# A two-layer decoder step: extra expert rows turned one chunk ahead, and the last layer's expert rows summed in PSUM

## The reference

```
x = x + y                                        # mixer
h = rms_norm(x, g_ffn)
gp = softmax(h @ w_rg + b_rg); g_val, g_idx = top_k(gp, 1)        # 1 of 4 groups
e_val, e_idx = top_k(softmax(logits of that group), 2)            # 2 of its 8 experts
act = silu(h @ w_gate[e]) * (h @ w_up[e]) * weight[e]             # D_EXPERT = 256
x = x + act @ w_down[e], summed over the two experts
...
y = x * rsqrt(mean(x * x) + 1e-6) * g_final      # after layer 1
```

## Time and profile before

| | us |
|---|---|
| median of three runs | 1174.64 (1173.73 to 1178.26) |
| the profiled execution's own time | 1172.26 |
| its span (first to last instruction) | 1170.5 |
| TensorE busy | 1029.1 (88%) |
| VectorE busy | 427.6 (37%) |
| granted TensorE clock, mean | 0.949 |

### The profile page before, as it was taken

The page is one execution under the profiler, slowest core; times in us unless marked ns, Lnnn a source line. Parts: engine busy times, 40 slices in busy tenths (PEclk is TensorE's granted clock), DMA queues, the critical chain, the costliest instruction groups (busy, mean ns, idle before and its releaser), DMA issues.

```text
span 1170.5 us, 19147 instructions
## 1 busy us (share of the span) xinstructions
PE 1029.1 (88%) x7027; PEld 653.9 (56%) x7028; DVE 427.6 (37%) x904; ACT 209.6 (18%) x425; POOL 183.3 (16%) x282
## 2 busy tenths in 40 slices
PE   5999998879899978788399999988999998899980
PEld 4888786545555544444177767644565554555540
DVE  2542002454721111111349899454462111112116
ACT  4000112232201110011230101163120111111112
POOL 1000010000043222121112120110013222222120
PEclk9999999989999998899799999999979999999995
DMA  9424032345489999999642200264068999999915
GB/s 358 203 102 158 1 125 74 135 189 209 156 295 409 408 409 409 409 409 414 280 182 73 72 1 1 62 257 162 18 256 289 406 407 403 390 402 408 382 70 230
DMA packets 73776, 281.61 MB, mean 241 GB/s; under 512 B 12830, under 2 KB 13406, under 8 KB 70304
## 3 DMA queue, kind: packets, MB, share of 16 engines
q1 hardware_dynamic: 56992, 251.53, 54.8%
q0 software_dynamic: 10960, 17.89, 4.4%
q10 hardware_dynamic: 5744, 11.10, 2.8%
HBM read 270.23 MB, written 29.65 MB: 256 GB/s over the span
## 4 chain that ended last, share of the span: by engine, by line
PE 62%; DMA 20%; DVE 12%; ACT 3%; issue 2%; ACTq 0%; POOLq 0%; SPq 0%; POOL 0%; DVEq 0%
DMA ring<-w_moe 12%; PE psum L2137 11%; PE psum L2041 7%; DMA ar<-w_moe 6%; PE psum L2198 6%; PE psum L1812 5%; PE psum L1768 5%; PE psum L2234 5%; DVE ar L1671 5%; PE psum L2259 3%; PE psum L1881 2%; DVE X L1395 2%; PE psum L2120 2%; PE psum L2167 2%; PE psum L1879 1%
## 5 line engine op out<-in xcount | busy, mean ns | idle before, releaser
L2137 PE MATMUL psum<-ring,ar 128*64 128x256 f32 x1408 | 176.9, 396 | 18.2 <-DMA ring<-w_moe 16.3
L2137 PEld LDWEIGHTS psum<-ring,ar 128*64 128x64 f32 x1408 | 101.7, 142 | 89.9 <-issue 26.3
L2234 PE MATMUL psum<-ar,ring 128*128 128x272 f32 x512 | 121.3, 398 | 5.3 <-DVE ar L1657 2.9
L2234 PEld LDWEIGHTS psum<-ar,ring 128*128 128x128 f32 x512 | 97.6, 192 | 30.2 <-issue 4.2
L1671 DVE SCALAR_TENSOR_TENSOR ar<-ar,sv 128x512 f32<-128x512 f32 x120 | 107.0, 893 | 5.8 <-ACT ar L1025 1.9
L1601 DVE COPY ar<-psum 128x128 f32<-128x128 f32 x64 | 18.7, 292 | 245.0 <-PE psum L2188 245.0
L2041 PE MATMUL psum<-ring,ar 128*128 128x512 f32 x192 | 90.6, 622 | 4.7 <-DVE ar L1385 4.7
L2137 PE MATMUL psum<-ar 128*64 128x256 f32 x640 | 81.5, 399 | 8.1 <-DMA ar<-w_moe 8.1
L2198 PE MATMUL psum<-ring,ar 128*64 128x512 f32 x352 | 84.1, 598 | 0.8 <-DVE ar L1601 0.4
L742 POOL DMA_INDIRECT expert_outputs<-ar,ixy x64 | 63.9, 998 | 55.4 <-POOL ixy L739 55.4
L2137 PEld LDWEIGHTS psum<-ar 128*64 128x64 f32 x640 | 45.9, 143 | 42.4 <-issue 12.1
(11 more groups left out here) (262 smaller groups left out, 1188.2 us busy)
## 6 DMA issues: line engine op xcount, KB each, us to landing
ring<-w_moe SPq DMA_DIRECT2D x44, 2048.0 KB, 16.6
ring<-w_moe SPq DMA_DIRECT2D x44, 1024.0 KB, 18.1
ar<-w_moe SPq DMA_DIRECT2D x20, 2048.0 KB, 16.5
ar<-w_moe SPq DMA_DIRECT2D x20, 1024.0 KB, 17.1
ring<-w_pw SPq DMA_DIRECT2D x6, 2048.0 KB, 10.6
ring<-w_mix SPq DMA_DIRECT2D x3, 3072.0 KB, 23.9
ring<-expert_outputs SPq DMA_DIRECT2D x8, 1024.0 KB, 7.8
ring<-kv_in SPq DMA_DIRECT2D x2, 2880.0 KB, 11.3
```

The costliest lines, as they stand in the source:

```text
L2137: t = mm(psum[64 * f:64 * f + 64, u % 2, 0:2 * P], xt[:, k, 64 * (u % 2):64 * (u % 2) + 64], w[:, k, f, :], start=k == 0, stop=k == KD - 1)
L2234: t = mm(psum[:, glu_bank(m) + h, 0:HALF], w[:, k, o:o + P], hT2[:, k, HALF * h:HALF * h + HALF], start=k == 0, stop=k == KD - 1)
```

## The change

Five edits are made together; the letters are those of the prediction, where D stands for two of them.

A. The loads of the start all go out on SP's queue, in the order in which they are used: tile 0, the identity, tile 1, the gains, tile 2, the first weights, tiles 3 and 4, further weights, and then the rest of constants and small vectors, which have semaphores of their own.

B and C. The rows of an extra chunk are turned one chunk ahead. The first chunk's are turned before job 1's products in each layer (`turn_more_rows(0)`), whether there is a chunk or not, and chunk c + 1's in the middle of chunk c. `keep_more_rows` is VectorE's part. Pool gathers one chunk further ahead and moves the clearing and the gather of the third pair of jobs behind the first chunk's. The chunk's intermediate tiles move to the router weights' place, its transposed product to another bank.

D. Before layer ends: Pool no longer copies an index where it is known when the program is built (the last eight jobs), ScalarE reads its counts ahead of the waits, and the fetch of tile 0 is split in two, with a semaphore for each half.

E. After layer 1, TensorE sums residual and expert rows in PSUM: identity times `X`, plus two diagonal matrices of the weights (made by VectorE) times the expert rows. ScalarE and VectorE read the sum there for the norm. Eighteen fill products stand ahead of the wait for `all_out`.

```
-            sp.dma_start(cst[:, :], consts).then_inc(consts_in, 16)
-            sp.dma_start(sv[:, :], smalls).then_inc(smalls_in, 16)
+            tokens_in(0)
+            sp.dma_start(cst[:, 0:C_SM], consts[:, 0:C_SM]).then_inc(ident_in, 16)
+            tokens_in(1)
+            sp.dma_start(sv[:, 0:V_GPK], smalls[:, 0:V_GPK]).then_inc(gains_in, 16)
+            tokens_in(2)
             sp.dma_start(ring[:, 0, 0:2 * D], w_mix0[0, :, 0:2 * D]).then_inc(later_w[0], 16)
+            tokens_in(3)
+            tokens_in(4)
...
@@ Pool, experts(n)
                 first_rows(1)
-                nc.gpsimd.memset(xg[2], 0.0).then_inc(moe.rows_clear, 1)
-                first_rows(2)
                 nc.gpsimd.memset(xe, 0.0).then_inc(pool_link, 1)
...
                 pool.indirect_dma_start(xe, None, xn_dram, ...).then_inc(ex[n].rows, 16)
+                nc.gpsimd.memset(xg[2], 0.0).then_inc(moe.rows_clear, 1)
+                first_rows(2)
                 rows_of(3, 6)
+                pool.wait_ge(ex[n].turned, 2)
+                nc.gpsimd.tensor_copy(ixe[0:JOB, 0:1], tg[0:JOB, MORE + 1:MORE + 2]).then_inc(ex[n].index, 1)
+                pool.wait_ge(ex[n].index, 2)
+                pool.indirect_dma_start(xe, None, xn_dram, ...).then_inc(ex[n].rows, 16)
...
-                            chunk_rows(before + c + 1)
+                            chunk_rows(before + c + 2)
                             chunk_out(before + c)
...
@@ Pool, outputs(it, u, known)
+                    if known:
+                        index = tb[:, MSLOTS * it + u:MSLOTS * it + u + 1]
+                        pool.wait_ge(moe.y_kept, MSLOTS * it + (EXPERTS * n + u + 1))
...
@@ SP, fetch(n)
+                    if i == 0:
+                        sp.dma_start(yg[0][:, 0:D], src[:, 0:D]).then_inc(first_rows_in, 16)
+                        sp.dma_start(yg[0][:, D:], src[:, D:]).then_inc(tile_in[0], 16)
...
@@ ScalarE, experts(n)
+                further_chunks, before_last = (act.value_load(...) for o in (EXPERTS - 1, 2 * EXPERTS - 1))
                 for b in range(3):
                     act.wait_ge(moe.y_out[b], 16 * (n + 1) * len(range(b, EXPERTS, 3)))
-                further_chunks, before_last = (act.value_load(...) for o in (EXPERTS - 1, 2 * EXPERTS - 1))
                 act.wait_ge(ex[n].out, 16 * (before_last + further_chunks) + 16)
                 act.sem_inc(moe.all_out, 1)
@@ VectorE
+                def keep_more_rows(chunk):
+                    dve.wait_ge(ex[n].turned, chunk + 2)
+                    nc.vector.tensor_tensor(xeT, psum[:, 7, :] ..., gains, ALU.mult).then_inc(ex[n].turns_kept, 1)
...
+                            if first and u == 1:
+                                keep_more_rows(0)
                             further(it, u - 1)
@@ TensorE, experts(n)
+                def turn_more_rows(chunk):
+                    pe.wait_ge(ex[n].rows, 16 * chunk + 16)
+                    pe.sem_inc(moe.seen, 1)
+                    rows_ = xe.rearrange("t (d k) -> t k d", k=KD)
+                    for k in range(KD):
+                        t = tr(psum[:, 7, JOB * k:JOB * k + JOB], rows_[:, k, :], ident[0:JOB, 0:JOB])
+                    t.then_inc(ex[n].turned, 1)
...
                             t.then_inc(ex[n].gu, 1)
+                            pe.wait_ge(moe.rows_kept, ...)
+                            turn_more_rows(before + c + 1)
                             pe.wait_ge(ex[n].act, before + c + 1)
...
                             t.then_inc(ex[n].down, 1)
+                            pe.wait_ge(ex[n].turns_kept, before + c + 2)
...
                             down_weights(it, u - 1)
+                            if first and u == 1:
+                                turn_more_rows(0)
+                                pe.wait_ge(ex[n].turns_kept, 1)
                             further(it, u - 1, 4 if jobs == MSLOTS else 1)
@@ TensorE, the end
+            def residual(i):
+                r = ROWS[i]
+                for h in range(2):
+                    mm(psum[0:r, 2 * (i % 4) + h, :], ident[0:r, 0:r], X[0:r, i, 512 * h:512 * h + 512],
+                       start=True, stop=False)
+            def expert_rows(i):
+                r = ROWS[i]
+                for k in range(2):
+                    if i == 0 and k == 0:
+                        pe.wait_ge(first_rows_in, 32)
+                    else:
+                        pe.wait_ge(tile_in[i], 48)
+                    pe.wait_ge(moe.combined, TILES + 2 * i + k + 1)
+                    for h in range(2):
+                        o = D * k + 512 * h
+                        t = mm(psum[0:r, 2 * (i % 4) + h, :], weight_diag(i, k), yg[i][0:r, o:o + 512],
+                               start=False, stop=k == 1)
+                t.then_inc(moe.last_sums, 1)
+            residual(0)
+            residual(1)
+            pe.wait_ge(moe.y_kept, 2 * EXPERTS)
+            residual(2)
+            stay_warm(18, 7)
+            pe.wait_ge(moe.all_out, 2)
+            residual(3)
+            for i in range(TILES - 1):
+                expert_rows(i)
+            pe.wait_ge(y_ready, 1)
+            residual(4)
+            expert_rows(4)
@@ VectorE, the end
-            update = combine(1)
-            update(0)
...
+                for k in range(2):
+                    nc.vector.tensor_scalar(weight_diag(i, k), ident[0:r, 0:r],
+                                            cw[0:r, ODD_ORDER.index(i), k:k + 1], None, ALU.mult
+                                            ).then_inc(moe.combined, 1)
...
-                nc.vector.scalar_tensor_tensor(out=view(D * i, D, parts=r), in0=X[0:r, i, :],
+                nc.vector.scalar_tensor_tensor(out=view(D * i, D, parts=r), in0=last_sum(i),
```

More of the change, by code:

```diff
@@ L702, in chunk_rows @@
                     pool.wait_ge(ex[n].turned, chunk + 1)
-                    o = nc.s_assert_within(chunk + MORE, MORE, 2 * MORE,
-                                           skip_runtime_bounds_check_because="at most MORE chunks and one empty")
-                    nc.gpsimd.tensor_copy(ixe[0:JOB, 0:1], tg[0:JOB, bass.ds(o, 1)]).then_inc(ex[n].ix, 1)
-                    pool.wait_ge(ex[n].ix, chunk + 1)
+                    o = nc.s_assert_within(chunk + MORE, MORE, 2 * MORE + 1,
+                                           skip_runtime_bounds_check_because="at most MORE chunks and two empty")
+                    nc.gpsimd.tensor_copy(ixe[0:JOB, 0:1], tg[0:JOB, bass.ds(o, 1)]).then_inc(ex[n].index, 1)
+                    pool.wait_ge(ex[n].index, 2 * chunk - 1)
                     pool.sem_inc(moe.seen, 1)
@@ L749, in body @@
                             rows_of(3 * it + (u // 2 + 4), u + 8)
-                        outputs(it, u)
+                        outputs(it, u, not gathers)
                 first_rows(0)
@@ L806, in _ @@
         def _(act):
-            for i in range(TILES):
-                act.dma_start(X[0:ROWS[i], i, :], x_in[P * i:P * i + ROWS[i], :]).then_inc(tile_in[i], 16)
             links = [0]
@@ L1390, in update @@
                     r = ROWS[i]
[L1391 removed]
+                    if i == 0:
+                        dve.wait_ge(first_rows_in, 16 * (n + 1))
+                    else:
+                        dve.wait_ge(tile_in[i], 16 * (n + 2))
                     for k in range(2):
+                        if i == 0 and k:
+                            dve.wait_ge(tile_in[0], 16 * (n + 2))
                         if k:
```

140 lines of the change are left out of this document (78 added, 62 removed).

## The result

The changed kernel takes 1183.2 us in the median (22 runs) against 1175.9 for the kernel before beside it (22 runs): a ratio of 1.0064, 95% interval 1.0047 to 1.0081, so 7.5 us (5.5 to 9.5) slower. Forecast was 1175.5 us, 0.9 us above the kernel before, with a range up to 1183.0. The time missed the range by 0.2 us. One of the 22 runs took 1812.6 us at a granted clock of 0.55; the ratio leaves it out, and without it the median is 1183.0, the very end of the range. The difference is clearer: the interval lies wholly above 1, and 0.64% is more than the 0.5% that the prediction took as the least that can be told from no change. "Same" had been its likeliest outcome.

The account below looks back on a forecast made before the run. The chain of waits was taken to run through TensorE nearly everywhere, with exceptions at the start, layer 0's expert weights and after each layer's experts. Terms -2.4 + 4.4 - 11.1 - 1.3 + 11.3 = +0.9 us gave 1175.5, range 1168.5 to 1183.0.

Parts of the forecast that it names:

- A: Start of the kernel: loads reordered on one queue bring the first projection sooner, -2.4 us (-4.5 to -0.5).
- B: Job 1 of both layers: turning the first extra rows there costs +2.4 and +2.0, together +4.4 us (+4 to +8).
- C: Layer 1's extra chunks: rows turned one chunk ahead make chunks shorter, -11.1 us (-13 to -9).
- D: End of layer 0: earlier register loads gain 1.06 us, the dropped index copy 0.25, the split fetch nothing; -1.3 us.
- E: End of layer 1: sums and fill on TensorE take 41.2 us after the last down products, +11.3 us (+10 to +12.5).
- Same: Outcome that the whole kernel's time cannot be told from no change, within about 0.5% (5.9 us); chance 0.72.
- rival 3: End of layer 1: the fill is hidden under the fetch, expert rows start 11.8 us earlier, 1163.7 us; chance 0.05.
- rival 2: Layer 1's chunks: their gain is lost to weights whose stream ends 9.6 us later than forecast, 1186.6 us; chance 0.05.
- ScalarE, not the DMA, sets the pace: Start, after tile 0's square: about 2.9 and 2.76 us to the third square, at 9.9 instead of 13.06 us.
- The price is what the same pair costs inside a chunk: 1.97 us: First turn before job 1, both layers: from first transpose to next product it takes 1.97 us, as in a chunk.
- Rival 1: Job 1 of both layers: TensorE waits on Pool's late gather, 6.5 us more than forecast, 1182.0 us; chance 0.10.
- Nothing gained, up to 0.4 lost: End of layer 0, split fetch: VectorE begins 1.2 us earlier, but its second tile comes no sooner, at about 578.6 us.

Follow-up runs that it names:

- e1: Changed kernel without its 18 fill products at the end of layer 1: 1174.2 us, ratio 0.9983 to the kernel before.
- e2: Changed kernel with the last layer's sums back on VectorE, the rest of the change kept: 1168.8 us, ratio 0.9945 to the kernel before.
- e6: Kernel before with the changed start alone, and tile 3 of X loaded ahead of the first weights: 1176.8 us (one run, beside 1178.2).
- e3: Changed kernel with TensorE's wait for the first extra rows' copy moved behind job 1's gate products: 1178.0 us, ratio 1.0022 to the kernel before.
- e4: Changed kernel with the first extra rows turned behind job 1's gate products: 1178.1 us, ratio 1.0034 to the kernel before.
- e5: Kernel of e2 with the first tile's rows fetched in one piece again, both layers: 1174.1 us, ratio 0.9970 to the kernel before.
- the three combined kernels: c1, c2 and c3: 1164.7, 1165.5 and 1160.0 us.
- e7: Changed kernel with fill products around the first turn of extra rows, two ahead and five behind: 1187.1 us, ratio 1.0114 to the kernel before.
- e8: The changed kernel measured again, unaltered, beside e7: 1180.4 us, ratio 1.0050 to the kernel before.
- c1: Changed kernel with last sums on VectorE, one-piece fetch, TensorE's copy wait behind job 1's gate products, tile 3 first: 1164.7 us, ratio 0.9900.
- c2: As c1, with Pool clearing the extra rows' buffer before it waits for the job table: 1165.5 us, ratio 0.9905 to the kernel before.
- c3: As c1, but with e4's order of the first turn in place of e3's: 1160.0 us, ratio 0.9886 to the kernel before.

## Why the prediction was wrong, point by point

- **E, the end of layer 1 (+11.3 forecast): right.** +11.2 and +10.7 in two profiles, 36 rows of fill, nothing idle on TensorE, first sum 22.1 us after the end of the last down products, where 22.7 was forecast; the last instruction ends 41.2 us after it, as forecast. e1 and e2 show the cause from both sides, and rival 3, a hidden fill, falls with them.
- **C, the chunks (-11.1): right.** Single chunks 7.06 us where 7.24 was forecast. The whole stretch from job 1's down products of layer 1 to the last is 11.9 and 10.2 us shorter. TensorE waits for no weights from 950 us on, so rival 2 falls.
- **A, the start (-2.4): mis-sized.** -1.15 and -1.47. The step that failed is "ScalarE, not the DMA, sets the pace". It was followed to tile 2 only, and there it held but for 0.8 us (10.70 us where 9.9 was forecast). Tile 3 behind 1 MB of weights was left out, and VectorE runs in order: a late reciprocal for tile 3 holds back tile 2's multiply. e6 moves that one load and gets -2.63. The term as a whole, -1.2 and -1.5, still lies in its own range (-4.5 to -0.5).
- On the Trainium skill's "Issuing engines are not separate DMA queues" (DMA: Bandwidth & Descriptors), weighed in the prediction as a possible result of nothing: e6's -2.63 us speaks against it as a rule about A. The order of the loads is what changed, and it was worth 2.3 to 2.8 us right (four profiles), 1.1 to 1.6 with one load too late (eight). That the queue they are issued from has a share in it is not excluded: no run changes it alone.
- **B, the first turn (+4.4): too small, the largest miss.** Layer 0 +3.7 and +3.5 (forecast 2.4), layer 1 +6.4 and +3.9 (forecast 2.0). The step that failed is "The price is what the same pair costs inside a chunk: 1.97 us". From the first transpose to the next product it was 3.25 us in layer 0 (330.47 to 333.72) and 3.02 in layer 1. In a chunk the next product follows the copy at once. Ahead of job 1 stand the register load of the chunk count and the branch, in TensorE's queue behind the wait, and with them it is 1.2 to 1.4 us from the copy's end to the product (e3). To it comes a gather a little late in layer 1 (0.6 us of waiting, where none was forecast; in layer 0 none, where 0.4 was), and in some executions the half clock behind the gap, 1.4 to 2.6 us. The part of B on which I was right is that layer 0's shift goes to the layer's end in full: +3.4 us at job 0's down products, +3.7 at the last (in e3 and e4, what was taken off there came back in part on the way). Rival 1 named the right place and the wrong wait: it is the copy and what is queued behind it, more than the gather.
- **D, the end of layer 0 (-1.3): did not arrive.** +0.1 and 0.0. The fetch was issued 0.85 us sooner after the last down products than before; it would have been 1.4, but the last output's DMA took 3.71 us instead of 3.15. Then the split, costed at "Nothing gained, up to 0.4 lost", made tile 1 late by as much: it landed 8.2 us after the first issue, where the prediction has 7.2 (571.38 to 578.6). Without the split, e5 and the three combined kernels are at -0.3 to -0.6 us, so the split is not all. In e3, e4 and e7 the split is kept and the last output's DMA takes 2.4 us; TensorE's first transposes come 1.3 to 1.4 us sooner than before, yet the first product only 0.4 to 0.6. What TensorE gained at its first transposes went in the fill behind them, as told under e5. The prediction had no such term: whatever came sooner for VectorE had still to pass through TensorE's queue.

Sum of the terms as measured in the quieter profile (e8): A -1.5, B +3.5 and +3.9, C -10.2, D 0, E +10.7, together +6.3 us, against medians of +7.5 and +5.9. The forecast of +0.9 had C and E right and lost 1 us on A, 3 on B and 1.3 on D. The range's upper end lay 8.4 us above the 1174.6 that it was made against. The measured difference, 7.5 us, is inside that, and the median of 1183.2 outside by 0.2, which is chance; but the likeliest value was wrong by 6.6 us, and "same" was wrong with it. The misses on A, B and D are of one kind: something queued in order behind what moved.

## What to carry over

A wait that is put ahead of a register load and a branch costs these too: price it from the wait's end to the next real instruction, not from the same pair elsewhere. When a load is moved in a queue, follow the chain past the first consumer, to the instruction that stands next in order on each engine. And fill products cost nothing only inside a wait whose length has been read; 18 of them ahead of the critical sums made 9.2 of the tail's 11.2 us.

## What the runs showed of the chip

The granted clock fell to half behind TensorE's gap at layer 1's job 1 in four of the six profiles in which it stood idle there for over 1 us (after, e1, e3, e5; not e2 and e8, which had the same 1.9 us gap as after). It fell in none of the seven in which it did not (before, e4, e6, e7, c1, c2, c3). In layer 0 it was e1 and e5 of five with the gap: the 20 products behind it took 3.94 us in e1 and 2.38 in the changed kernel. TensorE had also run at half clock in a stretch that ended 8 to 10 us ahead of the gap, for 3 us in e2 and some 6 in the others, e8 among them. So in these profiles the gap is needed and not sufficient. What else decides was not settled: after and e8 are the same kernel, once with the half clock behind the gap and once without.

The executions of one kernel also differ in stretches that no edit touches: in the 291 us between the two layers' experts, the 12 other profiles lay between -2.8 and +4.4 us of the kernel before's. A stage of one profile should be compared over several kernels before it is put down to an edit.
